# Second norm's row tiles and the attention heads' outputs: transposed by DMA instead of TensorE, with the head norm's vector multiplied into the output weights

## What is computed

```python
xn = rmsnorm(x, norm_mix_g)
u = xn @ w_in                                  # conv gates, q, k, v, merge gates
y_a = short_gated_conv(b_g, c_g, v_a, conv_w) @ w_a_out
o = diff_attention(q, k, v, lam, slopes)       # 4 heads, two softmax maps each, 128 columns a head
o = rmsnorm(o, subln_g) * (1.0 - lam_init)     # the head norm
y_b = o.reshape(B, S, 512) @ w_b_out
x = x + (g_a * y_a + g_b * y_b) @ w_o
h = rmsnorm(x, norm_mlp_g) @ w_mlp_in          # the second norm
x = x + square(relu(h)) @ w_mlp_out
return rmsnorm(x, norm_final_g)
```

## Time and profile before

| | us |
|---|---|
| median of 3 runs (lowest, highest) | 1221.82 (1221.73, 1221.93) |
| the profiled execution, its own time | 1218.94 |
| its span, slowest core (core 6) | 1217.4 |
| spans of all cores | 1213.7 to 1217.4 |
| TensorE busy / DVE / ACT / POOL | 1154.6 / 601.8 / 652.8 / 80.7 |

### The profile page before, as it was taken

One profiled execution on the slowest core, in us unless ns is written; L12 is line 12 of the kernel. 1 busy time (PEld: TensorE's weight loads), 2 busy tenths in 40 slices (PEclk: granted clock), 3 DMA queues, 4 the chain that ended last, 5 costly groups with the idle time before them and its releaser, 6 DMA issues.

```text
span 1217.4 us, 27397 instructions; the slowest of 8 cores (1213.7 to 1217.4 us)
## 1 busy us (share of the span) xinstructions
PE 1154.6 (95%) x7340; PEld 578.0 (47%) x7464; DVE 601.8 (49%) x971; ACT 652.8 (54%) x1055; POOL 80.7 (7%) x139
## 2 busy tenths in 40 slices
PE   3799999999999999999999999999999999999995
PEld 1455444555555555554444444444444444444443
DVE  2666436553444333333365337336455463727767
ACT  4555358889898998976746773330211112030065
POOL 0000012111110000010000000000000000000012
PEclk9999999999999999999999999999999999999998
DMA  8487320002000000049441408011230403030124
GB/s 174 157 192 190 65 36 2 2 3 37 3 2 3 2 2 2 3 65 199 119 104 27 114 3 140 15 35 24 47 53 17 70 1 70 1 70 10 27 87 191
DMA packets 16903, 71.90 MB, mean 59 GB/s; under 512 B 2128, under 2 KB 2384, under 8 KB 14320
## 3 DMA queue, kind: packets, MB, share of 16 engines
q0 software_dynamic: 6768, 35.65, 17.9%
q1 hardware_dynamic: 9840, 33.97, 8.1%
q10 hardware_dynamic: 144, 0.52, 0.1%
HBM read 97.40 MB, written 8.39 MB: 87 GB/s over the span
## 4 chain that ended last, share of the span: by engine, by line
PE 88%; DMA 3%; DVE 3%; issue 3%; ACT 2%; DVEq 0%; SPq 0%; ACTq 0%; POOL 0%; POOLq 0%
PE ps_all L290 68%; PE ps_all L287 11%; PE ps_all L292 7%; DMA big<-w_g 2%; PE ps_all L311 2%; ACT big L582 1%; DVE big L314 1%; DMA big<-xs 1%; ACT big L298 0%; DVE big L1102 0%; DVE big L1120 0%; PE ps_all L657 0%; DVE big L625 0%; DVE big L974 0%; DVE big L1090 0%
## 5 line engine op out<-in xcount | busy, mean ns | idle before, releaser
L290 PE MATMUL ps_all<-big 128*128 128x512 bf16 (+2 forms) x4068 | 901.3, 375 | 27.2 <-DVE big L314 13.4
L290 PEld LDWEIGHTS ps_all<-big 128*128 128x128 bf16 x4192 | 394.3, 98 | 484.1 <-issue 43.1
L582 ACT ACTIVATE big<-ps_all,big 128x1024 bf16<-128x1024 f32 (+3 forms) x428 | 324.8, 802 | 38.2 <-PE ps_all L287 14.6
L1075 ACT ACTIVATE big<-ps_all 128x512 bf16<-128x512 f32 x124 | 74.1, 598 | 334.0 <-PE ps_all L290 333.8
L1102 DVE TENSOR_TENSOR big<-ps_all,big 128x512 f32<-128x512 f32 x256 | 176.6, 691 | 39.5 <-PE ps_all L290 36.1
L287 PE MATMUL ps_all<-big 128*128 128x129 bf16 x2176 | 163.6, 221 | 3.9 <-DVE big L625 1.8
L287 PEld LDWEIGHTS ps_all<-big 128*128 128x128 bf16 x2176 | 126.8, 98 | 54.5 <-issue 45.7
L1076 DVE TENSOR_TENSOR big<-big 128x512 bf16<-128x512 bf16 x124 | 53.0, 427 | 162.0 <-ACT big L1075 162.0
L292 PE MATMUL ps_all<-big 64*128 64x512 bf16 (+3 forms) x640 | 108.7, 352 | 3.6 <-ACT big L582 2.3
L298 ACT ACTIVATE big<-big 128x1024 bf16<-128x1024 f32 (+1 forms) x65 | 68.7, 1056 | 60.1 <-PE ps_all L290 25.2
L314 DVE TENSOR_TENSOR big<-ps_all,big 128x1024 bf16<-128x1024 bf16 (+1 forms) x49 | 58.9, 1205 | 40.7 <-PE ps_all L311 40.7
(11 more groups left out here) (60 smaller groups left out, 416.8 us busy)
## 6 DMA issues: line engine op xcount, KB each, us to landing
big<-xs SPq DMA_DIRECT2D x48, 512.0 KB, 6.5
big<-w POOLq DMA_DIRECT2D x16, 1024.0 KB, 12.8
big<-w_g POOLq DMA_DIRECT2D x16, 512.0 KB, 7.9
out<-big SPq DMA_DIRECT2D x15, 512.0 KB, 2.6
big<-w_in POOLq DMA_DIRECT2D x12, 512.0 KB, 8.0
big<-w_o POOLq DMA_DIRECT2D x1, 2048.0 KB, 24.4
big<-w_a POOLq DMA_DIRECT2D x1, 1024.0 KB, 10.9
big<-w_b POOLq DMA_DIRECT2D x1, 1024.0 KB, 11.0
```

The source lines that it names most:

```text
L290: S.op("pe", lambda e: e.matmul(out, lhsT, rhs, start=start, stop=stop), reads=reads, writes=writes)
L582: S.op("act", lambda e, a=a, b=b, bi=bi: e.activation(PT[:, :, a:b], Sps[:, buf, :, a:b], AF.Exp, bias=btab[:, bi:bi + 1], scale=0.125), r ...
L1075: S.op("act", lambda e: e.activation(r, ph, AF.Relu), reads=[phk], writes=[rk])
```

## The change

The second norm: behind `row_scale` a DMA on SP's queue now turns the row tile (128 rows by 1024 columns of bf16, 256 KB) from SBUF to SBUF into `xn2T`, and one step later DVE multiplies `xn2T` in place by the norm's vector (`mul2`). ACT's squares go to two PSUM banks that nobody reads (`junk`), instead of onto the bf16 tile. The eight TensorE transposes and their PSUM banks are gone for this norm; the first norm keeps them.

The heads: `fin_` issues a DMA transpose (128 by 512, 128 KB) from `on` to `O_n`. The four TensorE transposes, the DVE instruction behind them and the planner's rules for flips are gone. The vector `gsub` is multiplied into `Wb` once, by one DVE instruction over 128x4096 bf16 behind the attention loop.

```diff
+    def turn_rows(xb, xbkey, dst, dkeys):
+        S.dma("sp", lambda e: e.dma_start_transpose(dst, xb), reads=[xbkey], writes=dkeys)
...
         def fin_():
-            flip_at[n] = LAT + dve(lambda e: e.tensor_tensor(
+            dve(lambda e: e.tensor_tensor(
                 on, o, ss[:, 4:8].unsqueeze(2).to_broadcast([128, 4, 128]), ALU.mult),
                 ["ato", "atrs"], [onk], 0.69, clk["pool"] + LAT)
+            i, h = steps[n]["i"], steps[n]["h"]
+            turn_rows(on.rearrange("p q v -> p (q v)"), onk,
+                      O_n[:, h, i * 512:(i + 1) * 512].rearrange("p (q t) -> p q t", q=4), ["qo%d_%d" % (i, h)])
-    def emit_flip(n):
...
-        for qc in range(4):
-            S.op("pe", lambda e, qc=qc: e.transpose(Tps[:, qc, :], on[:, qc, :], ident),
...
-        if flips and side["whole"] and flip_at.get(flips[0], BIG) <= t and b7["free"] <= t:
-            set_mode(0)
-            emit_flip(flips.pop(0))
-            continue
-        if flips and flip_at.get(flips[0], BIG) <= t and side["whole"]:
-            r_side = BIG
...
+    S.op("dve", lambda e: e.tensor_scalar_mul(Wb, Wb, gsub[:, 1:2]), reads=["Wb", "gsub"], writes=["Wb"])
...
-    pst_ring = Ring([bank_bf_T(6), bank_bf_T(7)], "pst", keys=["pb6", "pb7"])
+    junk = bank(6, 2)
+    S.reuse(["pb6"], ["pb7"])
...
-            rest_flips()
...
         if name == "act2":
             xb, xbkey = xb2_ring.next()
-            st2[T] = (xb, xbkey) + row_stats(x, "xm%d" % T, 128, xb, xbkey)
+            st2[T] = (xb, xbkey) + row_stats(x, "xm%d" % T, 128, junk, "pb6")
...
+        elif name == "post2":
             xb, xbkey, st, skey = st2[T]
-            flip_rows(xb, xbkey, 128, gmlp, "cst", xn2T_all[:, :, T * 128:(T + 1) * 128],
-                      ["xn2T_%d" % T, "ya%d" % i] + ["qo%d_%d" % (i, h) for h in range(4)], pst_ring)
+            xT = xn2T_all[:, :, T * 128:(T + 1) * 128]
+            turn_rows(xb, xbkey, xT, ["xn2T_%d" % T, "ya%d" % i] + ["qo%d_%d" % (i, h) for h in range(4)])
+        if name == "mul2":
+            xT = xn2T_all[:, :, T * 128:(T + 1) * 128]
+            S.op("dve", lambda e: e.tensor_tensor(xT, xT, gmlp.unsqueeze(2).to_broadcast([128, 8, 128]), ALU.mult),
+                 reads=["xn2T_%d" % T, "cst"], writes=["xn2T_%d" % T])
...
-            for name, off in (("act2", 0), ("dve2", 1), ("post2", 2)):
+            for name, off in (("act2", 0), ("dve2", 1), ("post2", 1), ("mul2", 2)):
...
-        for nm in ("post2", "dve2", "act2"):
+        for nm in ("mul2", "dve2", "post2", "act2"):
```

More of the change, by code:

```diff
@@ L295, in row_stats @@
     def row_stats(x, xkey, ntok, xb, xbkey):
+        xb = xb[:ntok]
         st, skey = stats[:ntok, stat_n[0]:stat_n[0] + 1], "stat%d" % stat_n[0]
         stat_n[0] += 1
-        S.op("act", lambda e: e.activation(xb[:ntok], x[:ntok], AF.Square, accum_out=st),
+        S.op("act", lambda e: e.activation(xb, x[:ntok], AF.Square, accum_out=st),
              reads=[xkey, "stat0s"], writes=[xbkey, skey])
@@ L514, in build_program @@
     OB_KEYS = ["pb4", "pb5", "pb6"]
-    Tps = bank(7).bitcast(BF16)[:, 0:512].rearrange("p (q t) -> p q t", q=4)
     S.op("dve", lambda e: e.memset(Ops[:, 2, 2, :], 1.0), writes=["pb6"])
@@ L615, in build_program @@
     o_free = [0.0, 0.0, 0.0]
-    flip_at = {}
     def evict_o(n):
@@ L646, in fin_ @@
         def fin_():
-            flip_at[n] = LAT + dve(lambda e: e.tensor_tensor(
+            dve(lambda e: e.tensor_tensor(
                 on, o, ss[:, 4:8].unsqueeze(2).to_broadcast([128, 4, 128]), ALU.mult),
                 ["ato", "atrs"], [onk], 0.69, clk["pool"] + LAT)
+            i, h = steps[n]["i"], steps[n]["h"]
+            turn_rows(on.rearrange("p q v -> p (q v)"), onk,
+                      O_n[:, h, i * 512:(i + 1) * 512].rearrange("p (q t) -> p q t", q=4), ["qo%d_%d" % (i, h)])
         yield (fin_, "pool")
-    def emit_flip(n):
-        st = steps[n]
-        i, h = st["i"], st["h"]
-        on, onk = at["on"][st["hid"] % 2], "aton%d" % (st["hid"] % 2)
-        for qc in range(4):
-            S.op("pe", lambda e, qc=qc: e.transpose(Tps[:, qc, :], on[:, qc, :], ident),
[L658 to L662, removed]
     b7 = dict(free=0.0)
@@ L793, in build_program @@
     chains, late = [], []
-    flips = []
     def set_mode(m):
@@ L887, in build_program @@
                 chains.append(dict(gen=chain(pv_n), next=None))
-                flips.append(pv_n)
             pv_n += 1
@@ L920, in load_x_mid @@
                   writes=["xm%d" % T])
[L923 to L926, removed]
     def gates_step(i, k):
@@ L1017, in do_ev2 @@
             row_scale(x, "xm%d" % T, 128, xb, xbkey, st, skey)
-        else:
+        elif name == "post2":
             xb, xbkey, st, skey = st2[T]
-            flip_rows(xb, xbkey, 128, gmlp, "cst", xn2T_all[:, :, T * 128:(T + 1) * 128],
-                      ["xn2T_%d" % T, "ya%d" % i] + ["qo%d_%d" % (i, h) for h in range(4)], pst_ring)
+            xT = xn2T_all[:, :, T * 128:(T + 1) * 128]
[4 more added lines that the diff above has]
+                 reads=["xn2T_%d" % T, "cst"], writes=["xn2T_%d" % T])
     ev2 = {}
@@ L1146, in build_program @@
             j += 1
+    S.reuse(["pb7"], ["pb6"])
     for g in range(1, 7):
```

## The result

The changed kernel takes 1258.54 us (median of 4 runs, 1257.73 to 1259.46) against 1221.88 of the kernel before on the same chip: a ratio of 1.0300, 95% interval 1.0282 to 1.0318. It is slower by 36.7 us; the prediction was +6.9, with a range that ended at 1244. The profiled execution took 1257.73 us, its span is 1256.2 us on core 4.

A forecast was written before the change was run, and what follows sets the result against it. TensorE's own work was taken to bound nearly everywhere. From 1218.9 us, -8.8 + 6.4 + 10.8 - 3.5 + 2.0 = +6.9 gives 1225.8; plus 2.9 to the runs' median, 1228.7 us; range 1214 to 1244, high ends 1249.6.

The forecast's parts named there:

- attention: Heads: 16 flips of four TensorE transposes go, 4.2 us in all; taken as -3.5 us, ends -4.2 and 0.
- L alone: Second norm: L, from a scaling's end until DVE can multiply, is 3.2 us without other traffic.
- the loop: Second norm: where DVE waits for the transpose, each z tile takes L + 1.88 us.
- the gain itself: TensorE spared: -8.8 us in the second norm (transposes 7.2, a wait 1.6), -3.5 us in the heads.
- the weights' scaling: Behind attention: scaling `Wb` takes 2.4 us, makes TensorE 3.2 us late, adds 2.0 us net (ends 0 and +5).
- Their transfers have many microseconds until the gates and idle engines: nothing.: Heads: DMA transposes of the heads' outputs finish well before the gates and cost nothing.
- L = 5.4 in full traffic: Second norm beside MLP weights: L grows by 2.2 us to 5.4; 4.3 for a tile at the edge.
- Rival 3: Second norm, later z tiles: transfers queue behind weights, L 8.3 us for three tiles, time 1238.5 us; chance 0.12.
- 0.2 us for two: Second norm: the two semaphore handoffs around a transpose add 0.2 us to its assumed 3.0 us.
- those of the other four stand ahead of gates or MLP steps, whose banks are others: Second norm: only the first four tiles' multiplications of each eight delay z tiles; the other four add nothing.
- The granted clock is no rival of its own.: z tiles: gaps of 2 to 4 us a tile were given no separate clock case; clock 1.00 with 2.3 us idle.
- Rival 4: Second norm: eight 128-column blocks transposed one after the other, L about 8 us everywhere, time 1260 us; chance 0.04.

The follow-up runs named there:

- gfin_late: The changed kernel with only the load of the final norm's vector put behind the last tile's transpose in SP's order: -7.5 us against the change, 1250.5 us.
- T8 mended: The changed kernel with W1's second and W2's first part made to wait for the last tile's product with the vector: 1247.7 us.
- the five places mended: The changed kernel with mT1's list shortened, one wait per engine, the product one tile later, and two MLP weight loads and `gfin` behind the last tile: 1202.2 us.

## Why the prediction was wrong

It had the right sign and mechanism, a DMA transpose that DVE waits for with the z additions behind it, and most of the sizes of the undisturbed case; it failed on what stands beside and ahead of the transfers.

- **Right: attention.** -3.5 predicted, -3.4 between the two slowest cores. That this agrees so closely is luck: from the first head's chain to the last, the medians of the eight cores are 4.9 us apart, above the term's end of 4.2.
- **Right: L alone and the loop.** "L = 3.2 alone": 3.3 to 3.4 for T1 to T3. "The loop is then L + 1.88 us a tile": 5.2 us, measured 5.2 to 5.26. DVE's multiplication from SBUF took 1.224 us, as assumed, and ACT's squares into PSUM 1.03. The landing of 3.0 us was as estimated. The rule of the Trainium skill in "Advanced Engine Details and Errata", X-Bar Transpose (TRN2), that transposing DMAs are as fast as ordinary ones, comes near for a transpose alone (3.0 us against 2.6 for a store of twice the bytes) and fails beside weights (16.3 and 24.3). The 1309 ns for one block in the Trainium skill, "VectorE: DVE Perf Modes", The three transpose paths, do not add up in series: eight blocks land in 3.0 us together.
- **Right: the gain itself.** Without the waits the norm's part was worth 7.8 us and the heads' 5.1; the prediction's terms were -8.8 and -3.5.
- **Too high: the weights' scaling.** L882 took 1.28 us, not 2.4, and TensorE waited 1.1 us there, not 3.2.
- **Wrong, 9.9 us: "Their transfers have many microseconds until the gates and idle engines: nothing."** Half of it was true: the turned tile was not wanted for long. But the engines were not idle (`w_g` and `w_o` were loading), the transfer took 24.3 us, and something else waited for it: the reuse of its source buffer, by a list of keys. The prediction followed who reads the result and not who must wait until the source is read.
- **Wrong, some 14 us: "L = 5.4 in full traffic".** The increase of 2.2 was taken from the loads of x rows. These move 4 KB packets, eight an engine; a transposed tile, which the prediction took to be written in 2-byte pieces, has 64 packets of 256 B an engine, and each waits its turn. T8's L was 19.7, 3.3 of them before the issue (next point). T9 and T10, put at 5.4 and 4.3, took 3.3 each: the weights had ended before T8 landed. Rival 3 named the mechanism at 8.3 us, from the wrong rows. The Trainium skill, "DMA: Bandwidth & Descriptors", section Queues, rings and completion order, says that a DMA engine changes between its queues packet by packet. The counts above agree with such turns (80 to 80, 190 to 176); whether a packet of the trace is what the page calls one, typically 9 to 17 descriptors, no run here shows. By it the number of packets was the thing to count, and no row of the kernel before had it for a transpose.
- **Wrong, 2 to 3 us each: "0.2 us for two" handoffs.** For the first tile of a block, and for the last head, SP worked through some 65 satisfied waits, 3.3 us. The recorder makes such lists in the kernel before too; of the transfers there only one, w_g, held TensorE up behind attention (1.8 us).
- **Wrong, 7.5 us: "those of the other four stand ahead of gates or MLP steps, whose banks are others".** T15's product is wanted by the MLP itself, and its transpose stood behind the 128 satisfied waits of the load of `gfin` on SP's queue; TensorE waited 6.5 us, and gfin_late gave 7.5. The prediction had followed DVE's list, and not SP's.
- **Wrong, some 9 us: "The granted clock is no rival of its own."** With waits of 16.9 us it was 0.52 over 760 to 780, and in four stretches the lower level cost the estimated 8.7 us above. It is a consequence of the waits: with T8 mended it was 1.00 there.

Rival 4 gave 1260, close to the time, by a mechanism that did not occur. The prediction's sum is right by its own terms, except for the high end: 1249.6 has T10 in full traffic, and with T10 at the edge, as in the forecast, it is 1247.4.

## What to carry to other kernels

A small-packet DMA put on a path beside bulk loads was not slowed here by a share of the bandwidth but by one large packet for each of its own: count its packets for each engine and either keep large loads out of its time by a real dependence, or leave enough slack behind it; here one more tile of slack alone gave back 25 of 37 us. Where work moves from TensorE to a DMA, read the issuing queue's own list (its waits, and what is ahead of it) and everything that the recorder lets wait for the source and target buffers, not only who reads the result. And a slow result need not condemn a change: with the five places mended the same change is 1.1% faster than the kernel before with the same short wait lists.

## What was not expected of the hardware

- Satisfied waits cost time: 50 ns each on SP, 65 of them 3.3 us and 128 of them 6.7; thinning them out in the kernel before, with nothing else changed, gave 5.6 us (0.9954, 0.9937 to 0.9972).
- Packets of two DMA queues came about one for one at 16 KB, 8 KB and 2 KB alike (80 to 80, 190 to 176, 192 to 223).
- Alone, a transpose's 1024 packets took 21 ns each and were through in less than 2 us of the 3.0 us to landing; beside weights the first came 5 to 6 us after the issue, with idle engines 1.2, which stays unexplained.
